# Reordered loads and write-outs around a neighbourhood attention loop, with three first score steps inside the last value unit

## The reference, cut to what matters

```
q = rms_norm_2(split_heads(h @ w_q), q_gain); k, kc likewise; v = split_heads(h @ w_v); vc = split_heads(hc @ w_v)
for each of 8 rows of a 64-wide token grid, 16 heads of 64 channels:
    s_loc = q_row . k_win * scale + bias        # window: 8 rows x 16 columns, clipped
    s_ctx = q_row . k_ctx * scale               # 256 context tokens
    p = softmax(concat(s_loc, s_ctx))
    out = p_loc . v_win + p_ctx . v_ctx
y = out @ w_o
```

## Time and profile before

| | us |
|---|---|
| median of 3 runs | 1702.45 (1700.41 to 1704.1) |
| profiled execution | 1702.61, of it the span of the profile 1700.6 |
| PE busy | 1642.9 (97% of the span) |
| DVE, ACT, POOL busy | 944.9, 758.6, 142.9 |

### The profile page before, as it was taken

One profiled execution on the slowest core, in us unless ns is written; L12 is line 12 of the kernel. 1 busy time (PEld: TensorE's weight loads), 2 busy tenths in 40 slices (PEclk: granted clock), 3 DMA queues, 4 the chain that ended last, 5 costly groups with the idle time before them and its releaser, 6 DMA issues.

```text
span 1700.6 us, 22020 instructions
## 1 busy us (share of the span) xinstructions
PE 1642.9 (97%) x8770; PEld 1396.5 (82%) x8770; DVE 944.9 (56%) x1184; ACT 758.6 (45%) x1062; POOL 142.9 (8%) x177
## 2 busy tenths in 40 slices
PE   6999999999999999999999999998889899999998
PEld 6888888889898788888887888997777788888887
DVE  5345554566555566656667667446874555335543
ACT  4234433234444355555554489436772433223320
POOL 3000000000000000000000000026760000000000
PEclk8999999999999999999999999999999899999999
DMA  8321123423323344466554223599633132333322
GB/s 255 95 73 52 50 75 99 143 99 131 100 100 124 99 128 129 141 209 181 176 162 128 67 68 106 183 275 241 169 94 99 50 99 83 102 99 99 91 86 83
DMA packets 263748, 205.86 MB, mean 121 GB/s; under 512 B 7827, under 2 KB 249854, under 8 KB 263662
## 3 DMA queue, kind: packets, MB, share of 16 engines
q1 hardware_dynamic: 249518, 165.03, 33.4%
q0 software_dynamic: 9152, 33.28, 5.8%
q10 hardware_dynamic: 4992, 6.34, 1.2%
HBM read 187.10 MB, written 20.66 MB: 122 GB/s over the span
## 4 chain that ended last, share of the span: by engine, by line
PE 85%; DVE 5%; ACT 4%; DMA 2%; SPq 1%; issue 1%; POOL 1%; ACTq 1%; POOLq 0%; DVEq 0%
PE ps L1649 27%; PE ps L1651 26%; PE ps L1650 26%; DMA gb<-bias_scr 2%; DVE w_lo L1059 1%; ACT w_hi L620 1%; PE ps L1779 1%; PE ps L2051 1%; ACT mod_tmp L743 1%; POOL sc L2184 1%; PE ps L1718 1%; ACTq L407 0%; PE ps L1765 0%; PE ps L2043 0%; PE ps L2044 0%
## 5 line engine op out<-in xcount | busy, mean ns | idle before, releaser
L1649 PE MATMUL ps<-h_hi,w_hi 128*128 128x512 f32 x960 | 376.9, 393 | 4.7 <-DVE h_lo L1473 2.5
L1650 PE MATMUL ps<-h_lo,w_hi 128*128 128x512 f32 x960 | 375.1, 391 | 0.0
L1651 PE MATMUL ps<-h_hi,w_lo 128*128 128x512 f32 x960 | 374.7, 390 | 0.0
L1059 DVE TENSOR_TENSOR w_lo<-w_raw,w_hi 128x2048 fp32r<-128x2048 f32 (+1 forms) x136 | 290.5, 2136 | 136.6 <-ACT w_hi L620 136.3
L620 ACT ACTIVATE w_hi<-w_raw 128x2048 fp32r<-128x2048 f32 (+1 forms) x136 | 242.4, 1782 | 136.5 <-PE ps L1651 117.8
L1649 PEld LDWEIGHTS ps<-h_hi,w_hi 128*128 128x128 f32 x960 | 181.0, 189 | 43.9 <-DVE w_lo L1059 3.2
L1651 PEld LDWEIGHTS ps<-h_hi,w_lo 128*128 128x128 f32 x960 | 180.9, 188 | 37.9
L1650 PEld LDWEIGHTS ps<-h_lo,w_hi 128*128 128x128 f32 x960 | 181.0, 189 | 36.4
L1649 PE MATMUL ps<-xg_hi,w_hi 128*128 128x512 f32 x352 | 139.5, 396 | 2.4 <-DVE w_lo L1059 2.4
L1651 PE MATMUL ps<-xg_hi,w_lo 128*128 128x512 f32 x352 | 137.3, 390 | 0.0
L1650 PE MATMUL ps<-a_lo,w_hi 128*128 128x512 f32 x352 | 137.1, 390 | 0.0
(11 more groups left out here) (325 smaller groups left out, 3025.2 us busy)
## 6 DMA issues: line engine op xcount, KB each, us to landing
mod_raw<-in_l_w_mod POOLq DMA_DIRECT2D x24, 1024.0 KB, 7.9
w_raw<-in_w_ffn_in SPq DMA_DIRECT2D x44, 512.0 KB, 5.0
w_raw<-in_l_ffn_w_up SPq DMA_DIRECT2D x44, 512.0 KB, 4.9
w_raw<-in_w_in SPq DMA_DIRECT2D x40, 512.0 KB, 5.1
w_raw<-in_l_na_w_qkv SPq DMA_DIRECT2D x24, 512.0 KB, 4.6
w_raw<-in_w_mem_kv SPq DMA_DIRECT2D x16, 512.0 KB, 4.1
qd<-q_scr SPq DMA_DIRECT2D x32, 256.0 KB, 4.6
w_raw<-in_w_ffn_out SPq DMA_DIRECT2D x16, 384.0 KB, 3.7
```

What stands on the lines that cost most here:

```text
L1059: v.tensor_tensor(wlo[s][:, 0:size], raw[s][:, 0:size], whi[s][:, 0:size].bitcast(F32), ALU.subtract).then_inc(w_lo, 1)
L1649: mm(o, w_h, x_h, start=first, stop=False, **kw)
L1650: mm(o, w_h, x_l, start=False, stop=False, **kw)
L1651: return mm(o, w_l, x_h, start=False, stop=last, **kw)
```

## The change

It has five parts. (1) ACT issues the write-outs of `vo_hi` one unit later, behind the weight split: unit 8's in iteration 9, unit 9's in 10, unit 10's in 11. (2) `vo_hi` and `vo_lo` get a second place for unit 11. Second `vo_hi` overlaps first `vo_lo`, so ACT waits for the low write-outs of unit 10 (and the last query write-out) before it writes unit 11's. (3) Score step 2 goes to bank 7 and is taken inside unit 11 with steps 0 and 1; its maximum and exp follow there. (4) SP's order: queries of head 2 and values of pair 1 ahead of unit 11's high write-out; then for head = 1 to 13 the queries of head + 2, the table of head + 3, the values; unit 11's low write-out is issued in two parts, four transfers after head = 1's loads and five after head = 2's. (5) `na_o` weight unit 2 is loaded after the loop's loads; two guards in `na_out` move to the heads whose place the tiles now lie in.

```diff
-        vo_hi = place("vo_hi", G + 4096, [P, 6, 256], F32R)
-        vo_lo = place("vo_lo", G + 5632, [P, 6, 256], F32R)
+        vo_hi = [place(f"vo_hi{b}", G + 4096 + 512 * b, [P, 6, 256], F32R) for b in range(2)]
+        vo_lo = [place(f"vo_lo{b}", G + 5632 + 512 * b, [P, 6, 256], F32R) for b in range(2)]
         def score_bank(g):
-            return (2 * (1 - v_last) + g) % 4
+            return 7 if g == 2 else (2 * (1 - v_last) + g) % 4
-        def spill_values(eng, i, x):
+        def spill_values(eng, i, x, taus=range(TT), context=True):
...
-            sp.wait_ge(evac, b + 12)
             sp.wait_ge(ns_ps, 4)
             load_queries(2)
+            load_values(1)
+            sp.wait_ge(evac, b + 12)
             spill_values(sp, 3, 0)
-            load_values(1)
-            sp.wait_ge(ns_ps, 8)
-            load_queries(3)
-            spill_values(sp, 3, 1)
-            na_o_unit(2)
-            for head in range(2, NA_HEADS - 2):
-                sp.wait_ge(bias_done, head + 1)
-                load_bias(head + 2, head % 2)
+            for head in range(1, NA_HEADS - 2):
                 sp.wait_ge(ns_ps, 4 * head + 4)
                 load_queries(head + 2)
+                if head + 3 < NA_HEADS:
+                    sp.wait_ge(bias_done, head + 2)
+                    load_bias(head + 3, (head + 1) % 2)
                 if head % 2 == 0:
                     a = head // 2 + 1
                     values_spilled(a // 2)
                     if a >= 3:
                         sp.wait_ge(no_ps, 2 * a - 2)
                     load_values(a)
+                if head == 1:
+                    spill_values(sp, 3, 1, range(2), False)
+                if head == 2:
+                    spill_values(sp, 3, 1, range(2, TT))
+            na_o_unit(2)
             na_o_unit(3)
...
                 if i >= 8:
+                    if i > 8:
+                        act.wait_ge(vo_done, 2 * (i - 8))
+                        spill_values(act, i - 9, 0)
                     if i == n - 1:
-                        na_exp(0)
-                        na_exp(1)
+                        for g in range(3):
+                            na_exp(g)
                     act.wait_ge(vc_ps, i - 7)
...
+                    if i == n - 1:
+                        act.wait_ge(v_spill_lo[2], V_SPILLED)
+                        act.wait_ge(q_spill_last, 32)
...
-                    if i < n - 1:
-                        act.wait_ge(vo_done, 2 * (i - 8) + 2)
-                        spill_values(act, i - 8, 0)
...
             for g in range(NA_G):
-                if g + 2 < NA_G:
+                if 2 < g + 2 < NA_G:
                     na_exp(g + 2)
...
                     na_max(0)
                     na_max(1)
+                    na_max(2)
...
-            na_max(2)
             for g in range(NA_G):
...
                         na_scores(0)
                         na_scores(1)
+                        na_scores(2)
...
                     pe.wait_ge(evac, b + n)
-                    na_scores(2)
                     na_scores(3)
```

More of the change, by code:

```diff
@@ L398, in values_of @@
             return 0 if a == 0 else 1 + (a - 1) % 2
-        def spill_values(eng, i, x):
+        def spill_values(eng, i, x, taus=range(TT), context=True):
             cols = slice(256 * i, 256 * i + 256)
-            src, done = ((vo_hi, v_spill_hi[i]), (vo_lo, v_spill_lo[i]))[x]
-            for tau in range(TT):
+            src, done = ((vo_hi[i // 3], v_spill_hi[i]), (vo_lo[i // 3], v_spill_lo[i]))[x]
+            for tau in taus:
                 to = v_scr[x, 256 * tau:256 * tau + 256, cols].rearrange("(q r w) f -> r w q f", q=4, r=2)
@@ L407, in spill_values @@
                     eng.dma_start(to[r], src[64 * r + span[tau]:64 * r + span[tau] + 32, 0:4, :].bitcast(F32)).then_inc(done, 16)
-            eng.dma_start(v_scr[x, 1024:1280, cols].rearrange("(q p) f -> p q f", p=P), src[:, 4:6, :].bitcast(F32)).then_inc(done, 16)
+            if context:
+                eng.dma_start(v_scr[x, 1024:1280, cols].rearrange("(q p) f -> p q f", p=P), src[:, 4:6, :].bitcast(F32)).then_inc(done, 16)
         def grid(x):
@@ L1006, in _ @@
                         act.wait_ge(evac, b + i)
-                    act.activation(vo_hi[:, 4:6, :], bank(4 + s).rearrange("p (q n) -> p q n", q=2), ACT.Copy).then_inc(vo_done, 1)
+                    if i == n - 1:
+                        act.wait_ge(v_spill_lo[2], V_SPILLED)
+                        act.wait_ge(q_spill_last, 32)
+                    to = vo_hi[(i - 8) // 3]
+                    act.activation(to[:, 4:6, :], bank(4 + s).rearrange("p (q n) -> p q n", q=2), ACT.Copy).then_inc(vo_done, 1)
                     act.wait_ge(pe_done, b + i + 1)
-                    act.activation(vo_hi[:, 0:4, :], v_banks(s), ACT.Copy).then_inc(vo_done, 1)
-                    if i < n - 1:
-                        act.wait_ge(vo_done, 2 * (i - 8) + 2)
-                        spill_values(act, i - 8, 0)
+                    act.activation(to[:, 0:4, :], v_banks(s), ACT.Copy).then_inc(vo_done, 1)
                 if i == 9:
@@ L1491, in na_out @@
                 dve.wait_ge(no_hi, head + 1)
-                if head == 0:
+                if head == 2:
                     dve.wait_ge(v_spill_hi[3], V_SPILLED)
+                if head == 8:
+                    dve.wait_ge(v_spill_lo[3], V_SPILLED)
                 rows = slice(64 * half, 64 * half + 64)
@@ L1572, in _ @@
                     dve.wait_ge(vo_done, 2 * (i - 8) + 1)
-                    low(vo_lo[:, 4:6, :], bank(4 + s).rearrange("p (q n) -> p q n", q=2), vo_hi[:, 4:6, :])
+                    to = (vo_lo[(i - 8) // 3], vo_hi[(i - 8) // 3])
+                    low(to[0][:, 4:6, :], bank(4 + s).rearrange("p (q n) -> p q n", q=2), to[1][:, 4:6, :])
                 if i >= 8:
@@ L1581, in _ @@
                 if i >= 8:
-                    low(vo_lo[:, 0:4, :], v_banks(s), vo_hi[:, 0:4, :]).then_inc(evac, 1)
+                    low(to[0][:, 0:4, :], v_banks(s), to[1][:, 0:4, :]).then_inc(evac, 1)
                 elif i < 4:
```

## The result

The changed kernel takes 1692.62 us (median of 6, 1689.4 to 1696.87) against 1703.16 for the kernel before on the same chip (median of 6): ratio 0.9942, 95% interval 0.9926 to 0.9958, some 10 us faster. A second set of runs gave 0.9937 (0.992 to 0.9953). The forecast was 1689.5 in a range of 1684.5 to 1697. Direction and range hold; the sum was 3 us too good, and one step in it was wrong. Each set of runs had the kernel before beside it on its own chip, with medians of 1703.16 here, 1701.52 for e1 to e4, 1700.94 for e5 to e8 and 1702.11 for e9 to e11. Medians of different sets therefore compare only within some 2 us; the ratios take this out.

A forecast was written before the change was run, and what follows sets the result against it. PE was taken as the bound almost everywhere, with stops of PE or POOL in the changed stretch. Gains of 1.2 + 1.2 + 6.8 + 3.9 = 13.1 us from 1702.61 gave 1689.5 us, range 1684.5 to 1697.

The forecast's parts named there:

- late write-outs: Rival, 0.12: unit 9's high write-outs run beside the loop's first loads, restart 2.8 us later; 9.1 us gain, 1693.5 us.
- The sign of being wrong that was named first: At PE's restart after unit 11: a restart after 1141 would show the forecast wrong; it expected 1139.5.
- Unit 10's late start: Start of unit 10: PE's 2.31 us delay and 1.8 us of low clock go, 4.1 us; unit 11 ends at 1134.7.
- The landing of unit 10's low write-outs: Before PE's restart: bound by bytes, landing at 1136.5, 0.5 us later than before; restart 1.2 us earlier.
- Third score step: Restart to normalise of step 2: about 2.5 us against 3.71, gain 1.2 us, bounds 0 and 2.
- Heads 2 to 4: Steps 9 to 17: SP's new order leaves 2.2 of 8.97 us excess, gain 6.8 us.
- the wait for queries at step 12: Heads 2 to 4: a rest of 1 to 2 us at step 12's scores or the table of head 4.
- Later heads: Steps 25 to 57: tables issued ahead of values end the stops at odd heads, gain 3.9 us, bounds 2.5 and 3.9.
- Full gain: Rival, 0.12: unit 10's write-outs land by 1134 and no loop load is late; 17.7 us gain, 1684.9 us.
- Slower: Rival, 0.04: values fill SP's queue, queries late at every head; slower than before at 174 GB/s, 1706.0 us at 160.

The follow-up runs named there:

- e1: Changed kernel with the high write-outs of units 9 and 10 issued right after their copies, only unit 8's behind the weight split; 1689.31 us, ratio 0.9926.
- e4: Changed kernel with the table of head + 3 issued behind the values of the same iteration instead of ahead; 1695.71 us, ratio 0.9966.
- e5: e1 with SP issuing unit 10's low write-outs before the values of pair 0 instead of behind them; 1689.27 us, ratio 0.9923.
- e8: Changed kernel with only score steps 0 and 1 inside unit 11, step 2 in the loop; 1693.06 us, ratio 0.9956.
- e9: Changed kernel with the edits of e1, e5 and e6 together; 1685.17 us (median of 5), ratio 0.9906.
- e11: The changed kernel run once more, unaltered, beside e9 and e10 on the same chip; 1691.27 us, ratio 0.9937.
- e7: Changed kernel with the na_o weight unit 2 load back inside the loop, behind the first four low write-outs; 1696.9 us, ratio 0.9972.
- e6: e1 with unit 11's high write-out cut: four transfers in place, five behind head 3's queries and head 4's table; 1688.33 us, ratio 0.9923.
- e2: Changed kernel with all three sets of high write-outs issued right after their copies, as in the kernel before; 1689.99 us, ratio 0.9935.
- e10: e9 with unit 8's high write-outs also issued directly, ahead of unit 10's weight split; 1688.58 us, ratio 0.9927.

## Why the prediction was right or wrong, point by point

**The number.** 1692.62 lies inside the stated range but just outside the forecast's own 1687 to 1692, and nearer to the rival *late write-outs* (1693.5, chance 0.12) than to 1689.5. From unit 8's copy to the last normalise the traces gained 8.5 and 9.7 us where 13.1 were forecast and 9.1 by that rival. The sign of being wrong that was named first, a restart after 1141, came: 1143.11. So the range holds because it was wide enough for the rival, not because the sum was right at the restart.

**Unit 10's late start: right.** The 2.31 us and the low clock went, and unit 11 ended as early as said: PE stopped at 1134.58, forecast 1134.7.

**The landing of unit 10's low write-outs, "I put their landing at 1136.5": wrong, and it is the step that failed.** Counted from the copy of unit 8 that is 50.5; it was 54.8 and 53.6. From the landing to the restart it took 3.0 us, as summed. So PE's restart, forecast 1.2 us earlier (1140.69 before, 54.7 from the copy), came 3.1 and 2.0 us later; with step 3's scores against step 3's, as in the table, 2.6 and 1.4. The step took the landing as fixed by the bytes. With the same bytes it moved from 54.8 to 50.4 (e1) and 45.1 (e5), so it was order and place. The cause, by the trace of the changed kernel and e1: unit 9's high write-outs behind the split. I had charged them with at most the bandwidth left idle while they waited. They started only 3.9 us later than before (20.2 against 16.3 us from the copy of unit 8) but landed 11.5 us later, while SP's loads for the loop were under way beside them. From issue to landing the 1.31 MB took 17 us, 77 GB/s where the pipes carried 260 in all. Before, they landed at 25.6; ACT's copy of unit 10's context part starts right then, at 1111.73 after 0.88 us idle, and the token part came 8.4 us later, when PE was done, so nothing hung on them:

```profile
1107.13 0.48 ACTq L408 DMA_DIRECT2D v_scr<-vo_hi  x1
...
1111.73 0.60 ACT L1007 ACTIVATE vo_hi<-ps 128x512 fp32r<-128x512 f32 x1 [0.88 <-issue]
```

The rival *late write-outs* had the mechanism and, with 2.8 us later, the price. The Trainium skill's rule that each transfer engine goes round the queues with work ("DMA: Bandwidth & Descriptors", Queues, rings and completion order) points the same way. I weighed it only as a delay of SP's loads; it was ACT's own write-outs, in a short queue beside a deep one, that came late. No run separates turn-taking from other contention.

A second thing stood behind it, which the prediction did not see: SP's list. Until 1124.45 SP was busy issuing the values of pair 0, so even a copy of unit 10 in time would have left the low write-outs behind them (e5 against e1: restart 2.3 us earlier).

**Third score step: 1.2 forecast.** From the restart to normalise 2 it took 2.72 us (1143.11 to 1145.83), forecast 2.5, before 3.71: 1.0 gained, or 1.5 against e8. At step 9 0.7 of it is left (e8).

**Heads 2 to 4: right, with two slips in the working.** 2.2 us were to be left, 1.3 and 1.6 were; the wait for queries at step 12 (1.11 us) is the one named (in the second trace PE stands 1.40 us there, and the profile names ACT's exp). The bytes of these heads add up to 4.1 MB, not 3.9, that is 276 GB/s and not 264, more than the 263 and 211 that it was held against. And 3.67 MB from 1140.7 on take until 1153.7, so the landing at 1155 to 1156.5 holds 1.3 us or more that the sum does not name; measured from the restart it was nevertheless right (16.8 us, forecast 15.5 to 17). That the weight unit makes it fit is shown by e7 (3.3 us of its 4.2). That the rest hangs on what is issued ahead of the queries is shown by e6; it takes 0.8 MB of write-outs from in front of them with the total unchanged, and does not separate issue time from bytes in front.

**Later heads: right.** 3.9 forecast, 62.7 - 58.9 = 3.8. The table's place is the cause (e4).

So the sum at step 9 was 2.4 us early and came out 2.2 us late (2.9 and 1.5 counted from unit 8's copy), and everything after it as forecast or better. *Full gain* needed write-outs landing by 1134; e9, a different kernel, has that (1131.2) and reaches 1685.2, where the rival said 1684.9. *Slower* fell: the pipes gave 244 and 247 GB/s where 174 was the turning point.

## What to carry to other kernels

Moving an issue a few us later can cost three times as many (3.9 became 11.5 here): ask what the other queues will be doing by then, and price the landing, not the issue. Where a restart has two suitors (PE and a landing), an edit that helps one is worth little until the other is early too, and two edits that each show little (e1, e5) must be tried together. On a list that issues transfers, put what is needed first at the front of the large ones: small tables before values, and what frees a buffer before what fills one.

## What the runs showed of the hardware

A 1.31 MB set of write-outs took 17 us from first issue to last landing in the changed kernel (260 GB/s in all in that stretch) and some 9 us in the kernel before (291 GB/s in all), where it was issued 3.9 us earlier. A stop of PE of 1.94 us at the restart was followed within 1.5 us by some 3 us at 1.2 GHz in two traces (before, e2) and by none in three (e5, e9, e10), so the length of the stop alone does not decide. In the changed kernel the clock fell during a stop of 8.53 us, 2.8 us after its start, and PE ran the first 4.6 us after it at 1.2 GHz. And part of the spread of a kernel's times lies far from any change: stretches at 1.2 GHz near 582 and 951 us in five traces of variants, which cost up to 1.7 us each, and near 949 us alone in three.
